# Weight products of 512 columns issued as two products of 256 columns in a decoder-layer kernel

## What is computed

```
h = rms_norm(x, norm_mix)
p = h @ w_in                        # 2048 x 9752: queries, keys, values (3608 columns), gates (3 x 2048)
y_c, y_b, y_a = three token mixers  # sparse attention, stick-breaking, sliding window; 512 wide each
m = sum_i sigmoid(gate_i) * (y_i @ w_branch_i)
x = x + m @ w_out                   # 2048 x 2048
h = rms_norm(x, norm_ffn)
x = x + (silu(h @ w_gate) * (h @ w_up)) @ w_down    # 2048 x 5632, 2048 x 5632, 5632 x 2048
out = rms_norm(x, norm_final)
```

## Time and profile before

| | |
|---|---|
| median of 3 runs | 1399.41 us |
| the profiled execution's own time | 1400.08 us |
| its span | 1398.4 us |
| granted TensorE clock, mean | 0.998 |
| TensorE, matmul records | 7344, of them 3936 of 512 columns |
| TensorE busy | 1386.4 us (99%) |
| VectorE busy | 923.2 us (66%) |
| ScalarE busy | 701.9 us (50%) |
| weights and other data moved | 260.58 MB, 186 GB/s |

### The profile page before, as it was taken

The page is one execution under the profiler, slowest core; times in us unless marked ns, Lnnn a source line. Parts: engine busy times, 40 slices in busy tenths (PEclk is TensorE's granted clock), DMA queues, the critical chain, the costliest instruction groups (busy, mean ns, idle before and its releaser), DMA issues.

```text
span 1398.4 us, 18555 instructions
## 1 busy us (share of the span) xinstructions
PE 1386.4 (99%) x7344; PEld 1172.5 (84%) x7344; DVE 923.2 (66%) x1189; ACT 701.9 (50%) x912; POOL 45.4 (3%) x70
## 2 busy tenths in 40 slices
PE   9999999999999999999999999999999999999997
PEld 8999977777788888888888989888888898888886
DVE  5455557657655657666788888874446788887554
ACT  7333356656545655465645555543334455545443
POOL 4000000000000110000000000000000000000111
PEclk9999999999999999999999999999999999999999
DMA  7777755545565667556566665565666575667653
GB/s 239 247 217 219 216 140 150 149 139 148 150 184 164 188 200 213 174 164 201 157 182 204 213 184 177 184 216 193 191 185 179 182 221 164 192 190 228 207 188 115
DMA packets 135233, 260.58 MB, mean 186 GB/s; under 512 B 8448, under 2 KB 25408, under 8 KB 134768
## 3 DMA queue, kind: packets, MB, share of 16 engines
q1 hardware_dynamic: 133328, 251.89, 59.7%
q0 software_dynamic: 1792, 7.57, 1.5%
q10 hardware_dynamic: 32, 0.01, 0.0%
HBM read 257.33 MB, written 2.10 MB: 186 GB/s over the span
## 4 chain that ended last, share of the span: by engine, by line
PE 94%; DVE 3%; DMA 1%; ACT 1%; issue 1%; SPq 0%; ACTq 0%; DVEq 0%
PE bank L628 25%; PE bank L629 25%; PE bank L630 25%; PE bank L867 5%; PE bank L869 5%; PE bank L870 5%; PE bank L619 2%; DVE weight_lo_ring L1259 1%; DMA raw_ring<-in_w_up 1%; PE bank L766 1%; PE bank L677 1%; DVE weight_sums_lo L1279 0%; ACT weight_hi_ring L1029 0%; DMA x<-in_x 0%; DVE weight_sums L1268 0%
## 5 line engine op out<-in xcount | busy, mean ns | idle before, releaser
L1259 DVE TENSOR_TENSOR weight_lo_ring<-raw_ring,weight_hi_ring 128x1024 fp32r<-128x1024 f32 (+2 forms) x480 | 581.3, 1220 | 326.6 <-ACT weight_hi_ring L1029 273.0
L1029 ACT ACTIVATE weight_hi_ring<-raw_ring 128x1024 fp32r<-128x1024 f32 (+2 forms) x432 | 448.7, 1051 | 363.4 <-PE bank L630 297.2
L628 PE MATMUL bank<-weight_hi_ring,hT_hi 128*128 128x512 f32 (+2 forms) x768 | 303.3, 395 | 0.0
L629 PE MATMUL bank<-weight_lo_ring,hT_hi 128*128 128x512 f32 (+2 forms) x768 | 296.9, 387 | 0.0
L630 PE MATMUL bank<-weight_hi_ring,hT_lo 128*128 128x512 f32 (+2 forms) x768 | 296.8, 386 | 0.0
L628 PEld LDWEIGHTS bank<-weight_hi_ring,hT_hi 128*128 128x128 f32 x768 | 145.0, 189 | 31.2 <-issue 6.5
L630 PEld LDWEIGHTS bank<-weight_hi_ring,hT_lo 128*128 128x128 f32 x768 | 145.0, 189 | 27.2
L629 PEld LDWEIGHTS bank<-weight_lo_ring,hT_hi 128*128 128x128 f32 x768 | 145.2, 189 | 24.6
L628 PE MATMUL bank<-weight_hi_ring,h2T_hi 128*128 128x512 f32 x352 | 139.6, 397 | 0.6 <-DVE weight_lo_ring L1259 0.5
L629 PE MATMUL bank<-weight_lo_ring,h2T_hi 128*128 128x512 f32 x352 | 139.1, 395 | 0.0
L628 PE MATMUL bank<-weight_hi_ring,actT_hi 128*128 128x512 f32 x352 | 139.0, 395 | 0.0
(11 more groups left out here) (238 smaller groups left out, 1736.5 us busy)
## 6 DMA issues: line engine op xcount, KB each, us to landing
raw_ring<-in_w_in SPq DMA_DIRECT2D x96, 512.0 KB, 3.6
raw_ring<-in_w_gate SPq DMA_DIRECT2D x88, 512.0 KB, 4.5
raw_ring<-in_w_up SPq DMA_DIRECT2D x88, 512.0 KB, 4.3
raw_ring<-in_w_down SPq DMA_DIRECT2D x88, 512.0 KB, 4.6
raw_ring<-in_w_in SPq DMA_DIRECT2D x56, 452.0 KB, 4.2
raw_ring<-in_w_out SPq DMA_DIRECT2D x32, 512.0 KB, 4.6
raw_ring<-in_w_br_c SPq DMA_DIRECT2D x16, 256.0 KB, 4.7
raw_ring<-in_w_br_a SPq DMA_DIRECT2D x16, 256.0 KB, 7.4
```

The lines of the kernel that those rows point to most:

```text
L628: pe.matmul(dst, x_hi, w_hi, start=first and k == 0, stop=False)
L629: pe.matmul(dst, x_hi, w_lo, start=False, stop=False)
L1029: act.activation(whi[:, s, :, 0:width(u)], raw[:, s, :, 0:width(u)], ACT.Copy).then_inc(hi_ready, 1)
L1259: dve.tensor_tensor(lo, w, hi.bitcast(F32), ALU.subtract).then_inc(lo_ready, 1)
```

## The change

In `products`, where the width is 512, the columns are cut into (0, 256) and (256, 512), and the loop over blocks and tiles gets the halves as its innermost index. Each half does the same three matmuls on its 256 columns of the same bank. Only the first half of the first block carries `start=True`, as in the up units. Narrower products (452 and 444 columns) stay one product. Nothing else is changed: order of units, waits, signals, loads and the other engines.

```
             def products(slot, lhs, pair, first, last, k0, width=W, tiles=tuple(range(TT))):
 
                 l_hi, l_lo = lhs
-                for k, t in [(k, t) for k in range(UK) for t in tiles]:
-                    dst = bank[2 * pair + t][:, 0:width]
+                parts = [(0, Q4), (Q4, W)] if width == W else [(0, width)]
+                for k, t, (a, b) in [(k, t, part) for k in range(UK) for t in tiles for part in parts]:
+                    dst = bank[2 * pair + t][:, a:b]
                     x_hi, x_lo = (m[:, k0 + k, t * P:(t + 1) * P] for m in (l_hi, l_lo))
-                    w_hi, w_lo = (m[:, slot, k, 0:width] for m in (whi, wlo))
-                    pe.matmul(dst, x_hi, w_hi, start=first and k == 0, stop=False)
-                    pe.matmul(dst, x_hi, w_lo, start=False, stop=False)
-                    m = pe.matmul(dst, x_lo, w_hi, start=False, stop=last and k == UK - 1)
+                    w_hi, w_lo = (m[:, slot, k, a:b] for m in (whi, wlo))
+                    opening = first and k == 0 and a == 0
+                    pe.matmul(dst, x_hi, w_hi, start=opening, stop=False, skip_group_check=True)
+                    pe.matmul(dst, x_hi, w_lo, start=False, stop=False, skip_group_check=True)
+                    m = pe.matmul(dst, x_lo, w_hi, start=False, stop=last and k == UK - 1, skip_group_check=True)
                 return m
```

## The result

| | before | after |
|---|---|---|
| median | 1399.09 us (1397.33 to 1399.76, 4 runs) | 1406.68 us (1405.79 to 1408.23, 4 runs) |
| ratio | | 1.0058, 95% interval 1.0045 to 1.0070 |
| span of the profiled execution | 1398.4 us | 1405.2 us |

The change makes the kernel slower by 0.58%, clear of the 0.2% that a measurement can tell. The forecast was 1379 us; the time is that of rival 1 (1406 us), inside the range given, and on the other side from the forecast.

A forecast was written before the change was run, and what follows sets the result against it. TensorE's queue of matmuls was taken as the bound. From 1400.08 us, 21.7 us came off for cheaper halves and 1.0 went back for waits: 1379.4, said as 1379 us; range 1375 to 1407 us.

The forecast's parts named there:

- rival 1: All halves everywhere run at the dear pace, 117.1 or 117.9 ns: 1406 or 1412 us; chance 0.23.
- rival 3: TensorE's instruction supply cannot sustain the halves' pace; at 135 ns a half it costs 148 us: 1547 us; chance 0.04.
- rival 4: In the feed-forward gates, late VectorE or loads give the 6.4 us gain back: 1385 us; chance 0.05.
- the price of a half: Each 256 column matmul in all cut products costs 113.5 ns, so two take 227.0 ns.
- 15.3 us of expected gain: Mixers' gates, branches, w_out and w_down: 2880 products go from 232.3 to 227.0 ns, 15.3 us less.
- 6.4 us forecast: Feed-forward gates: 1056 products go from 233.1 to 227.0 ns, 6.4 us less.
- Rows 7 and 8: Profile rows of dearer halves: 117.1 ns in a seven unit, 117.9 ns in plain up units 6 and 7 before w_down.
- Rival 2: Dear pace only around w_down: 1056 matmuls at 235.8 instead of 227.0 ns, 9.3 us lost, 1388 us; chance 0.18.
- The seven units: Feed-forward units of 21 matmuls of 256 columns, 117.1 ns each; as up units, forecast to stay unchanged.
- the 1 us that I had taken back: Feed-forward first block and restart after w_down: shorter gate units wait longer for VectorE, 1 us of gain lost.

The follow-up runs named there:

- the first experiment: Changed kernel with 192 unused bytes before hT_hi and 832 before merged, putting hT and actT at h2T's distance: 1381.81 us, ratio 0.9870.
- the kernel with the sums moved: Changed kernel with 192 and 832 unused bytes, plus ext_hi and ext_lo (weight sums) 960 bytes further up: 1387.47 us, and 1381.19 us once more on another chip.

## Why the prediction was wrong

**The costs before the change were right.** 232.4, 232.3 and 233.1 ns for a whole, 3936 of them, and the stages' sums moved by about what the paces say. The counts came out as forecast (11280). No wait and no supply of instructions became a bound: rival 3 is out, as w_down keeps 118.6 ns for hundreds of pairs, and rival 4 stayed small, TensorE waiting 4.0 us for low parts instead of 3.3.

**The step that failed is the price of a half.** I took 113.5 ns from the plain up units, because "the plain units differ in nothing of the instructions". They differed from 2880 of the 3936 products in one thing that I had listed and not weighed: the stationary is h2T there, and hT, actT or yT here. At hT's and actT's place the pace is 118.7. So 15.3 us of expected gain became a loss of 12.4 (gates of the mixers, branches, w_out and w_down in the table). For the 1056 products of the feed-forward gates the row was the right one: 6.4 us forecast, 4.4 measured. Of the 2 us missing the 13 units that ran at 117.7 are 1.4 (13 x 24 x 4.4 ns).

**The warning was in the rows.** Rows 7 and 8 were dearer, and I set them aside, one for a reason and one without. The earlier trace rows is the second rhythm, at the very distance that is quick elsewhere: its units lie among the first w_down units, and in the kernel after, with w_down in halves around them, the same units ran at 113.3. The earlier trace rows has the sums of h2 as stationary, at distance 896, and a product whose two operands lie at distance 0. A dearer pace that identical instructions show, unexplained, was worth more than 0.23. It said that something outside the instructions sets the price, and whether that something is the same in the stages to be changed could have been read from the tiles' addresses.

**Rival 1 was right in time and half right in mechanism.** It spoke of some cost that is there in nearly all stretches; it is there by place, in w_down, w_out and the mixers' gates, and not in the feed-forward gates. That its time fits is luck: it had all halves at 117.1 ns for +7.0 us, and what was measured is a loss of 12.4 us at 118.7 less a gain of 4.4 at 114.0, with smaller terms. Rival 2 had a dear pace in w_down right (117.9 ns against 118.7), and missed that the mixers' gates and w_out share it.

**The seven units** were to stay, and took 1.7 us more. The trace has the place: the 11 starts that follow the second seven unit of a block, each the first of a gate unit, come 2.1 us later in all, and inside the seven units nothing grew (130.6 and 130.3 us). There the profile puts the wait down to VectorE's low part; it was 0.8 us before gate units in the earlier trace rows, and now is

```profile
PEld bank L630 <- DVE weight_lo_ring L1261: 4.0, 12, 1.1
```

with 3.2 of the 4.0 us before these gates. The waits of the up units in the earlier trace rows (2.5 us) are gone. So this is the 1 us that I had taken back, near its place; VectorE was full there. That a quicker VectorE would return it was not tested.

**A rule of the Trainium skill** ("TensorE: Matmul & The Clock Gate", the section on 56 ns and 53.3 ns) had said slower for another reason, a fixed 2.5 ns for each matmul, by which I had estimated 1410 us. Its time is near, its mechanism is not what the runs show: with the same 3936 added matmuls the kernel takes 1381.8 or 1421.2 us, by the distance.

## What to carry to other kernels

Where each matmul of 256 columns has its own load of 128 stationary columns, 113.3 ns was the best pace here, and it was missed by 4 to 7 ns through where the two operands lie. Compare their starts within 512 bytes and try some distances; the padding costs only its bytes (1024 in each partition here). When a price is taken from a row of the same form, check also that its tiles lie as the new ones will. Two paces for identical instructions mean that a price has a second argument: find it before the sum is made.

The version that beats both kernels is the first experiment's: the change with 192 and 832 unused bytes, 1381.8 us, 1.3% under the kernel before. It depends on the quick rhythm. Its own four executions lay within 1.4 us, but the kernel with the sums moved took from 1381.2 to 1392.9 us.

## What the runs showed of the hardware

- The start-to-start time of a load and a 256 column matmul depends on the distance between the stationary and the moving operand in a partition: 113.3 ns at best, 117.3, 117.7, 118.7 or 120.0 otherwise. 64 bytes of shift of both changes none of these. Operands of 512 columns feel about 1 ns of it, those of 452 as much at one distance (206.7 ns with hT at 896, 64, 0 and 320, 205.6 at 960), those of 444 up to 3 ns (198.9 at 896, 200.0 at 0, 202.2 at 64). The physical reason was not found. The Trainium skill ("TensorE: Matmul & The Clock Gate", the step-by-step section) says that loading the next stationary does not take read bandwidth from the running matmul, as the two have their own read ports. The runs show that where loads and matmuls are this dense the pace of the pair is not independent of where the two lie; whether read bandwidth is the reason no run shows.
- At odd multiples of 64 bytes two rhythms exist, 113.3 and 117.7 ns, each kept through a whole w_down phase (48 units). In w_down they changed only where the stream of matmuls was broken; between feed-forward gates and seven units they also changed without a break. The same program took either: its two traced plain executions differ by 7.7 us. Yet in the 152 units before the feed-forward part five traces of four kernels have the same units in the same rhythm.
